# Gate stage of a two-block transformer step: two of four column groups of a scaled residual turned by VectorE block transposes in place of TensorE transposes

## The chip, the cores and the metric

The kernel runs on one core of a Trainium2 chip. The metric is the device time of one execution in microseconds; smaller is better. The times are medians of several runs. The profile is of one execution, taken by the hardware profiler.

## What is computed

The reference is two transformer blocks over a sequence of 256 positions of width 2048, in float32. The change lies in the last step of the first block, and in the norm with which the second block begins:

```python
# h: [1, 256, 2048] after the feed-forward of the first block
gate = jax.nn.sigmoid(rms_norm(h, norm_ple[i]) @ ple_w_gate[i])   # 2048 x 2048
h = h + (p[i] @ ple_w_proj[i]) * gate
...
x = rms_norm(h, norm_final)          # end of the first block
...
h = rms_norm_2(x, norm_g[i, 0])      # start of the second block
q, k, v = split_cols(h @ w_in, SWA_SPLITS)
```

`rms_norm` divides each row by the root of its mean square and multiplies by a gain for each column.

## The kernel before

**Precision.** A float32 product is made of three products of a shorter format: each weight piece `raw` is split into `whi` (a copy rounded by ScalarE, L2049) and `wlo = raw - whi` (VectorE, L1246), each activation into a high and a low half in the same way. TensorE then adds hi x hi, hi x lo and lo x hi (L604, L605, L606).

**Weight stream.** All weights come through one stream of 756 pieces of 128 x 1024 (512 KB), loaded by the SP queue into four slots (`SLOTS = 4`). A raw slot is loaded again once `wlo` of its piece is made (`lo_ready`). ScalarE's copy of a piece waits for its load and for TensorE to have used the piece four before (`piece_used`). VectorE's subtraction waits for ScalarE's copy (`hi_ready`), and TensorE waits for VectorE's (`lo_ready`) at a piece's first matmul.

**Order.** Each engine runs its own list of instructions in the order in which it is written. `rows_body` on VectorE and on ScalarE goes through a stage's pieces. In step q it splits piece q, then does what the dictionary `between` holds for q - LEAD (`LEAD = 3`), and then, on VectorE, if q - LEAD is the last piece of a group, it evacuates the group's two PSUM banks.

**The gate stage.** `rows_group` multiplies the 256 tokens (two tiles of 128) with 512 columns of `ple_w_gate` at a time: four column groups f, each of 8 pieces, each piece with 12 matmuls of 128 x 512. After group f ScalarE makes the sigmoid (`gate_sigmoid`), and VectorE's `gate_in` does three operations for each token tile: the sigmoid times the projection (L1795), plus the residual (L1796), and times the gain of the final norm into `xN` (L1798, it counts `ple_gain`). ScalarE then takes squares of both.

**Turning.** The next stage wants `xN` with the columns on the partitions. So each 128 x 512 column group of `xN`, with its two token tiles, is transposed to four tiles of 128 columns x 256 tokens. In the kernel before TensorE does this for all four groups, eight transposes each (`turn_gate`, `turn_rows`, L619), into four PSUM banks; group f - 1 is turned in the middle of gate group f. ScalarE (`tiles_hi`, L2087) and VectorE (`tiles_lo`, L1364) scale the turned tiles from PSUM by the second block's gain and split them into the halves of `H`. The next stage's values and keys are products with `H`.

The stage ahead, the last feed-forward product (`fd`), turns its column groups for f < 3 in another way: VectorE's `turn_quarters` moves 32 x 32 blocks from `xN` into `z`, 16 instructions in two lots of eight (L1373), one after the split of piece 8f + 11 and one after that of 8f + 12. `turned_hi` (L2093) and `turned_lo` (L1380) make the halves from `z`.

Of the kernel before, what the change touches and what calls it, by code (L numbers as in the profile page):

```python
# [209 lines left out]
def program(nc, xT, pT, wstream, consts, setup, params, grows, xrows, out):  # L210
# [11 lines left out]
    with ExitStack() as ctx:  # L222
        def sb(name, shape, dt=F32):
            return ctx.enter_context(nc.sbuf_tensor(name, shape, dt))

        def sem(name):
            return ctx.enter_context(nc.semaphore(name))
# [7 lines left out]
        H = sb("H", [P, CH, 2, S], FR)  # L235
# [88 lines left out]
        def gain(name, t):  # L324
            return par[:, ds(PO[name][0] + t, 1)]
# [4 lines left out]
        def part(buf, t, h):  # L330
# [45 lines left out]
        fd_sq, fd_turned, fd_hi, a2_ready = (sem(n) for n in ("fd_sq", "fd_turned", "fd_hi", "a2_ready"))  # L376
        grs_ready, ple_x, ple_gain, ple_sq, ple_turned, ple_hi, a3_ready = (
            sem(n) for n in ("grs_ready", "ple_x", "ple_gain", "ple_sq", "ple_turned", "ple_hi", "a3_ready"))
# [51 lines left out]
        def nsa_probs(n, e):  # L430

            _, _, e0, e1, probs = nsa_block(n)
            return probs.rearrange("p (r k b c) -> p r b k c", r=(e1 - e0) // 2, b=2, c=P // 2)[:, (e - e0) // 2, e % 2, :, :]
# [40 lines left out]
        def swa_out(buf, n, part):  # L474

            g, t, _, _, _ = swa_block(n)
            return buf[:, HPG * g:HPG * g + HPG, part, t * P:t * P + P]
# [37 lines left out]
        def _(pe):  # L515
# [74 lines left out]
            def rows_group(p, p0, u, u0, K, src, ready=None, between={}, upper=False, free=False):  # L590

                for t in range(QT):
                    if not free:
                        pe.wait_ge(z_ready, u + t + 1)
                for k in range(K):
                    if ready:
                        pe.wait_ge(*ready(k))
                    if k % 2 == 0:
                        pe.wait_ge(lo_ready, p + (k // 2 + 1))
                    s, w = (p0 + k // 2) % SLOTS, slice(k % 2 * WIDE, k % 2 * WIDE + WIDE)  # L600
                    for t in range(QT):
                        tok = slice(t * P, t * P + P)
                        bank = psum[(u0 + t) % 4 + (4 if upper else 0)]
                        nc.tensor.matmul(bank[:, :], src[:, k, 0, tok], whi[:, s, w], start=(k == 0), stop=False)  # L604
                        nc.tensor.matmul(bank[:, :], src[:, k, 0, tok], wlo[:, s, w], start=False, stop=False)  # L605
                        last = nc.tensor.matmul(bank[:, :], src[:, k, 1, tok], whi[:, s, w], start=False, stop=(k == K - 1))  # L606
                    if k % 2 == 1:
                        last.then_inc(piece_used, 1)
                        if k // 2 in between:
                            between[k // 2]()  # L610

            def turn_rows(f, lo_done, turned):

                if f:
                    pe.wait_ge(lo_done, 4 * f)
                for d in range(4):
                    for t in range(QT):
                        c = (4 * f + d) * P
                        last = nc.tensor.transpose(psum[4 + d][:, t * P:t * P + P], xN[:, t, c:c + P], ident)  # L619
                    last.then_inc(turned, 1)  # L620
# [356 lines left out]
            def turn_fd(f):  # L977

                pe.wait_ge(z_ready, 4 + UB["fd3"] + 2 * f + 2)
                turn_rows(f, a2_ready, fd_turned)  # L980
# [13 lines left out]
            def turn_gate(f):  # L994

                pe.wait_ge(ple_gain, 2 * f + 2)
                turn_rows(f, a3_ready, ple_turned)
            for f in range(4):
                rows_group(PB["gate"] + 8 * f, PB["gate"] + 8 * f, UB["gate"] + 2 * f, UB["gate"] + 2 * f, DT, A,
                           lambda k: (a2_ready, k + 1), {3: lambda: turn_gate(f - 1)} if f else {0: lambda: turn_fd(3)})  # L1000


            natural(PB["v2"], UB["v2"], H, {5: lambda: turn_gate(3)}, ready=lambda k: (a3_ready, k + 1))
# [236 lines left out]
        def _(dve):  # L1240
# [105 lines left out]
            def rows_body(p, p0, per, groups, evac, between={}, short=0, ahead={}, halves=()):  # L1346

                for q in range(LEAD, per * groups + AHEAD):
                    if q in ahead:
                        ahead[q]()  # L1350
                    if AHEAD <= q < per * groups + AHEAD - short:
                        split_lo(p + q, (p0 + q) % SLOTS, WIDE if q in halves else PW)
                    if q - LEAD in between:
                        between[q - LEAD]()
                    f, done = divmod(q - LEAD + 1, per)
                    if f and f <= groups and done == 0:
                        dve.wait_ge(piece_used, p + (SLOTS + q - LEAD + 1))
                        evac(f - 1)

            def tiles_lo(dst, name, f, hi_sem, ready):  # L1360

                for d in range(4 * f, 4 * f + 4):
                    dve.wait_ge(hi_sem, d + 1)
                    V.scalar_tensor_tensor(dst[:, d, 1, :], psum[4 + d % 4][:, 0:S], gain(name, d), dst[:, d, 0, :].bitcast(F32),  # L1364
                                           ALU.mult, ALU.subtract).then_inc(ready, 1)
# [10 lines left out]
            def turned_lo(dst, name, f, hi_sem, ready):  # L1376

                for d in range(4 * f, 4 * f + 4):
                    dve.wait_ge(hi_sem, d + 1)
                    V.scalar_tensor_tensor(dst[:, d, 1, :], z[:, d % 4, :], gain(name, d), dst[:, d, 0, :].bitcast(F32),  # L1380
                                           ALU.mult, ALU.subtract).then_inc(ready, 1)
# [70 lines left out]
            def nsa_lo(n):  # L1452

                g, t, _, _, _ = nsa_block(n)
                dve.wait_ge(nsa["o_hi"], 2 * g + 2 - t)
                V.tensor_tensor(swa_out(H, n, 1), psum[4 + t][:, :].rearrange("p (r q) -> p r q", r=HPG),
                                swa_out(H, n, 0).bitcast(F32), ALU.subtract).then_inc(nsa["o_ready"], 1)
# [303 lines left out]
            def fd_lo(f):  # L1761

                if f < 3:
                    turned_lo(A, "g_ple", f, fd_hi, a2_ready)
                else:
                    tiles_lo(A, "g_ple", f, fd_hi, a2_ready)
# [23 lines left out]
            def gate_in(f):  # L1790

                w = slice(f * WIDE, f * WIDE + WIDE)
                for t in range(QT):
# [3 lines left out]
                    dve.wait_ge(ple_x, 2 * f + t + 1)  # L1797
                    V.tensor_tensor(xN[:, t, w], yN[:, t, w], gfrow[:, w], ALU.mult).then_inc(ple_gain, 1)  # L1798

            def gate_lo(f):  # L1800

                tiles_lo(H, "g0", f, ple_hi, a3_ready)
            dve.wait_ge(in_gf, 16)
            rows_body(PB["gate"], PB["gate"], 8, 4, gate_in,
                      {2: lambda: fd_lo(3), 3: norm_gate, **{8 * f + 5: lambda f=f: gate_lo(f - 1) for f in range(1, 4)}})

            def norms_k2():

# [11 lines left out]
            def rows_k2():  # L1820

                take_rs(3, 4)
                V.tensor_scalar(rs2b, rs[:, :], float(HD) ** -0.5, None, ALU.mult).then_inc(rs_ready, 1)
            values(PB["v2"], UB["v2"], 0, nrs, {AHEAD + 1: lambda: gate_lo(3), AHEAD + 3: norms_k2})
            body(PB["k2"], PB["k2"], UB["k2"], UB["k2"], ZB["k2"], ZB["k2"], 4, DT, between={NORM_AT["k2"]: rows_k2})

# [212 lines left out]
        def _(act):  # L2039
# [35 lines left out]
            def rows_body(p, p0, it, pieces, between={}, short=0, halves=()):  # L2075

                for q in range(LEAD, pieces + AHEAD):
                    if AHEAD <= q < pieces + AHEAD - short:
                        split(p, p0, q, pieces, it, WIDE if q in halves else PW)
                    if q - LEAD in between:  # L2080
                        between[q - LEAD]()

            def tiles_hi(dst, name, f, turned, hi_sem):

                for d in range(4 * f, 4 * f + 4):
                    act.wait_ge(turned, d + 1)
                    C.activation(dst[:, d, 0, :], psum[4 + d % 4][:, 0:S], ACT.Copy, scale=gain(name, d)).then_inc(hi_sem, 1)  # L2087

            def turned_hi(dst, name, f, turned, hi_sem):

                act.wait_ge(turned, 4 * f + 4)
                for d in range(4 * f, 4 * f + 4):
                    C.activation(dst[:, d, 0, :], z[:, d % 4, :], ACT.Copy, scale=gain(name, d)).then_inc(hi_sem, 1)  # L2093
# [60 lines left out]
            g0, g1 = PO["g_mix"]  # L2154
# [197 lines left out]

            def gate_hi(f):

                tiles_hi(H, "g0", f, ple_turned, ple_hi)
            rows_body(PB["gate"], PB["gate"], 0, 32, {
                0: lambda: fd_squares(3), 1: lambda: fd_hi_of(3), 3: lambda: root(3, nrs, nvar),
                **{8 * f + 7: lambda f=f: gate_sigmoid(f) for f in range(4)},
# [129 lines left out]
            for c, n in enumerate(CHUNKS2):  # L2488
# [22 lines left out]
                else:  # L2511
# [6 lines left out]
                    for q in range(2 * n):  # L2518
                        if 2 <= q and q + LEAD < 2 * n:
                            split(PB[dn], PB[dn], q + LEAD, 0, 0)  # L2520
                        f, h = divmod(q, n // 2)
# [281 lines left out]
```

## Time and profile before

| | us |
|---|---|
| median of 3 runs | 2203.51 |
| lowest, highest | 2202.99, 2204.32 |
| the profiled execution | 2202.45 |
| its span in the profile | 2200.6 |
| TensorE busy | 2188.3 |
| VectorE busy | 1517.5 |
| ScalarE busy | 1123.5 |
| GpSimd busy | 628.7 |

The span runs from the first instruction of the program to the last; the execution's time holds 1.85 us around it. The gate stage stands at 1103.9 to 1194.6 us. Matmuls overlap in the engine, so the distance of their starts is the measure of TensorE's pace, and not their durations. In a row of a timeline, what stands in brackets is how long the engine was idle before, and what ended that.

### The profile page before, as it was taken

The numbers are of one execution on the slowest core, as the hardware profiler recorded it, in microseconds if no ns is written. First come the engines' busy times: TensorE is split into PE (matmuls) and PEld (weight loads), VectorE is DVE, ScalarE is ACT, GpSimd is POOL, SyncE is SP. The second block draws the span as 40 slices with busy tenths as digits, with TensorE's granted clock in tenths as the row PEclk, the third lists the DMA queues.
The fourth block names the chain that finished last, engine by engine and source line by source line (L and its number), as shares of the span: only waits on it lengthen the run. The fifth ranks groups of instructions, "written<-read, shape, count | busy, mean of one in ns | idle before, by whom it ended". The sixth has DMA issues, their size and how long they took to land.

```text
span 2200.6 us, 34123 instructions
## 1 busy us (share of the span) xinstructions
PE 2188.3 (99%) x11565; PEld 1870.8 (85%) x11565; DVE 1517.5 (69%) x2075; ACT 1123.5 (51%) x1690; POOL 628.7 (29%) x573
## 2 busy tenths in 40 slices
PE   9999999999999999999999999999999999999998
PEld 8888988888888888888888887888888888888887
DVE  6877765558658757755966666577774688756875
ACT  6445555555445445454556455465553455434553
POOL 3202320361362363153000133006540255303431
PEclk9999999999999999999999999999999999999999
DMA  7665335456555556555555653545555555555554
GB/s 253 232 228 170 107 133 187 169 185 213 189 186 206 191 181 209 201 200 191 186 187 192 220 174 134 198 157 187 194 191 194 188 191 191 191 191 191 189 209 147
DMA packets 118079, 414.28 MB, mean 188 GB/s; under 512 B 12897, under 2 KB 18049, under 8 KB 117473
## 3 DMA queue, kind: packets, MB, share of 16 engines
q1 hardware_dynamic: 111600, 401.37, 53.2%
q10 hardware_dynamic: 6384, 11.70, 1.7%
q8 instruction: 54, 0.88, 0.2%
q14 instruction: 41, 0.33, 0.0%
HBM read 409.29 MB, written 2.15 MB: 187 GB/s over the span
## 4 chain that ended last, share of the span: by engine, by line
PE 93%; POOL 2%; issue 2%; DVE 2%; ACT 1%; DMA 0%; POOLq 0%; DVEq 0%; ACTq 0%
PE bank L547 31%; PE bank L555 16%; PE bank L1207 4%; PE bank L1205 4%; PE bank L1206 4%; PE bank L881 4%; PE bank L882 4%; PE bank L883 4%; PE bank L605 3%; PE bank L606 3%; PE bank L604 3%; POOL bias L2544 1%; PE bank L660 1%; PE bank L661 1%; PE bank L662 1%
## 5 line engine op out<-in xcount | busy, mean ns | idle before, releaser
L1246 DVE TENSOR_TENSOR wboth<-raw,wboth 128x1024 fp32r<-128x1024 f32 x756 | 963.9, 1279 | 542.1 <-ACT wboth L2049 541.0
L2049 ACT CAST wboth<-raw 128x1024 fp32r<-128x1024 f32 x756 | 780.4, 1041 | 585.6 <-PE bank L1207 126.5
L547 PE MATMUL bank<-A,wboth 128*128 128x512 f32 x2928 | 705.4, 392 | 0.5 <-DVE wboth L1246 0.3
L547 PEld LDWEIGHTS bank<-A,wboth 128*128 128x128 f32 x2928 | 536.9, 188 | 105.2 <-issue 1.2
L555 PEld LDWEIGHTS bank<-A,wboth 128*128 128x128 f32 x2928 | 376.7, 191 | 14.8
L555 PE MATMUL bank<-A,wboth 128*128 128x256 f32 x2928 | 384.0, 283 | 0.0
L2544 POOL TENSOR_TENSOR PT<-z,rs 128x256 f32<-128x256 f32 x88 | 73.4, 835 | 465.8 <-DVE z L1277 465.2
L2544 POOL TENSOR_TENSOR bias<-z,rs 128x256 f32<-128x256 f32 x64 | 104.5, 1633 | 199.1 <-DVE z L1277 109.7
L1277 DVE TENSOR_REDUCE z<-bank 128x256 f32<-128x512 f32 x172 | 118.0, 687 | 28.2 <-PE bank L547 27.9
L1205 PE MATMUL bank<-wboth,H 128*128 128x512 f32 x352 | 136.9, 389 | 0.0
L1206 PE MATMUL bank<-wboth,H 128*128 128x512 f32 x352 | 136.9, 389 | 0.0
L1207 PE MATMUL bank<-wboth,H 128*128 128x512 f32 x352 | 136.9, 389 | 0.0
L881 PE MATMUL bank<-wboth,H 128*128 128x512 f32 x312 | 121.5, 389 | 1.2 <-DVE wboth L1246 1.2
L882 PE MATMUL bank<-wboth,H 128*128 128x512 f32 x312 | 121.4, 389 | 0.0
L883 PE MATMUL bank<-wboth,H 128*128 128x512 f32 x312 | 121.4, 389 | 0.0
L2262 ACT ACTIVATE Sm<-bias 128x256 f32<-128x256 f32 x64 | 26.7, 418 | 170.7 <-POOL bias L2544 170.7
L2630 POOL TENSOR_TENSOR x<-x,Sm 128x512 f32<-128x512 f32 x18 | 35.4, 1991 | 206.8 <-DVE x L1749 137.5
L2669 POOL TENSOR_TENSOR bias<-Sm 128x256 f32<-128x256 f32 x44 | 71.9, 1633 | 38.0 <-DVE Sm L1971 37.7
L2544 POOL TENSOR_TENSOR kT<-z,rs 128x256 f32 (+1 forms) x12 | 11.3, 942 | 249.9 <-DVE z L1277 249.9
L547 PE MATMUL bank<-H,wboth 128*128 128x512 f32 x320 | 79.1, 394 | 0.0
L1206 PEld LDWEIGHTS bank<-wboth,H 128*128 128x128 f32 x352 | 66.1, 188 | 13.8
L1207 PEld LDWEIGHTS bank<-wboth,H 128*128 128x128 f32 x352 | 66.1, 188 | 13.7
(340 smaller groups left out, 3090.3 us busy)
## 6 DMA issues: line engine op xcount, KB each, us to landing
raw<-wstream SPq DMA_DIRECT2D x756, 512.0 KB, 3.3
bias<-bias_rows ACTq DMA_DIRECT2D x6, 512.0 KB, 6.1
x<-xrows ACTq DMA_DIRECT2D x1, 2048.0 KB, 10.6
bias<-grows ACTq DMA_DIRECT2D x2, 1024.0 KB, 7.2
out<-x SPq DMA_DIRECT2D x8, 256.0 KB, 2.1
x<-xT SPq DMA_DIRECT2D x7, 256.0 KB, 5.4
pA<-bias_rows ACTq DMA_DIRECT2D x2, 512.0 KB, 8.8
Sm<-grows ACTq DMA_DIRECT2D x1, 1024.0 KB, 6.7
```

The costliest lines, as they stand in the source:

```text
L547: last = nc.tensor.matmul(bank(j)[:, :], whi[:, s, cols(i)], moving(j, k), start=(k == 0), stop=(k == K - 1))
L555: last = nc.tensor.matmul(bank(j)[:, 0:S], wlo[:, s, cols(i)], moving(j, k)[:, 0, :], start=False, stop=False)
L881: nc.tensor.matmul(bank[:, :], a_hi, w_hi, start=start, stop=False)
L882: nc.tensor.matmul(bank[:, :], a_hi, w_lo, start=False, stop=False)
L883: return nc.tensor.matmul(bank[:, :], a_lo, w_hi, start=False, stop=stop)
L1205: nc.tensor.matmul(bank[:, :], H[:, k, 0, tok], whi[:, s, w], start=(k == 0), stop=False)
L1206: nc.tensor.matmul(bank[:, :], H[:, k, 0, tok], wlo[:, s, w], start=False, stop=False)
L1207: return nc.tensor.matmul(bank[:, :], H[:, k, 1, tok], whi[:, s, w], start=False, stop=(k == n - 1))
L1246: V.tensor_tensor(wlo[:, s, 0:w], raw[:, s, 0:w], whi[:, s, 0:w].bitcast(F32), ALU.subtract).then_inc(lo_ready, 1)
L1277: V.tensor_reduce(dst(j) if dst else z[:, (z0 + j) % 4, :], bank[:, :].rearrange("p (h c) -> p c h", h=2), AX, ALU.add).then_inc(z_ready, 1)
L2049: C.copy(whi[:, s, 0:w], raw[:, s, 0:w]).then_inc(hi_ready, 1)
L2544: return lambda zz: G.tensor_tensor(dst, zz, by, ALU.mult)
```

## The change

The column groups f = 0 and 1 of the gate stage are turned by VectorE as in the stage ahead. TensorE's turns of these two go, its turns of groups 2 and 3 stay in their places, as does the turn of the feed-forward's fourth group (`turn_fd(3)`). VectorE gets two lots of eight block transposes for each of the two groups. ScalarE and VectorE read `z` for these groups in place of PSUM. `turned_hi` waits for all four tiles of a group at once.

```diff
@@ the tensor engine's list
             for f in range(4):
                 rows_group(PB["gate"] + 8 * f, PB["gate"] + 8 * f, UB["gate"] + 2 * f, UB["gate"] + 2 * f, DT, A,
-                           lambda k: (a2_ready, k + 1), {3: lambda: turn_gate(f - 1)} if f else {0: lambda: turn_fd(3)})
+                           lambda k: (a2_ready, k + 1), {0: {0: lambda: turn_fd(3)}, 3: {3: lambda: turn_gate(2)}}.get(f, {}))
@@ the vector engine's list
+            def gate_turn(f, i0):
+
+                if i0 == 0:
+                    dve.wait_ge(ple_gain, 2 * f + 2)
+                if f and i0 == 0:
+                    dve.wait_ge(a3_ready, 4 * f)
+                turn_quarters(f, i0, ple_turned)
+
             def gate_lo(f):
 
-                tiles_lo(H, "g0", f, ple_hi, a3_ready)
+                if f < 2:
+                    turned_lo(H, "g0", f, ple_hi, a3_ready)
+                else:
+                    tiles_lo(H, "g0", f, ple_hi, a3_ready)
             dve.wait_ge(in_gf, 16)
             rows_body(PB["gate"], PB["gate"], 8, 4, gate_in,
-                      {2: lambda: fd_lo(3), 3: norm_gate, **{8 * f + 5: lambda f=f: gate_lo(f - 1) for f in range(1, 4)}})
+                      {2: lambda: fd_lo(3), 3: norm_gate, **{8 * f + 8 + i: lambda f=f, i=i: gate_turn(f, 2 * i) for f in range(2) for i in range(2)}, **{8 * f + 5: lambda f=f: gate_lo(f - 1) for f in range(1, 4)}})
@@ the scalar engine's list
             def gate_hi(f):
 
-                tiles_hi(H, "g0", f, ple_turned, ple_hi)
+                if f < 2:
+                    turned_hi(H, "g0", f, ple_turned, ple_hi)
+                else:
+                    tiles_hi(H, "g0", f, ple_turned, ple_hi)
```

How the instructions stand, first on TensorE behind the twelfth piece of the gate stage (piece 11). `con` holds the identity, `x` is the memory of `xN`, `bank` a PSUM bank, `wboth` the split weights. Before:

```order
2582 L606 MATMUL bank<-wboth,A 128x512
2583 L619 MATMUL bank<-con,x 128x128 [waits ple_gain]
2584 L619 MATMUL bank<-con,x 128x128 x7
2585 L604 MATMUL bank<-wboth,A 128x512 [waits lo_ready,a2_ready]
2586 L605 MATMUL bank<-wboth,A 128x512
```

and now:

```order
2581 L605 MATMUL bank<-wboth,A 128x512
2582 L606 MATMUL bank<-wboth,A 128x512
2583 L604 MATMUL bank<-wboth,A 128x512 [waits lo_ready,a2_ready]
2584 L605 MATMUL bank<-wboth,A 128x512
2585 L606 MATMUL bank<-wboth,A 128x512
```

The eight transposes have gone from between two pieces; the matmul behind them, which waits for the split of its piece, stays.

On VectorE, behind the evacuation of gate group 0, whose last operation is L1798. Before:

```order
758 L1798 TENSOR_TENSOR x<-y,bias 128x512 [waits ple_x]
759 L1246 TENSOR_TENSOR wboth<-raw,wboth 128x1024 [waits hi_ready] x6
760 L1364 SCALAR_TENSOR_TENSOR H<-bank,par,H 128x256 [waits ple_hi] x4
761 L1246 TENSOR_TENSOR wboth<-raw,wboth 128x1024 [waits hi_ready] x2
```

and now:

```order
758 L1798 TENSOR_TENSOR x<-y,bias 128x512 [waits ple_x]
759 L1246 TENSOR_TENSOR wboth<-raw,wboth 128x1024 [waits hi_ready]
760 L1373 STREAM_TRANSPOSE z<-x 32x8x32 [waits ple_gain]
761 L1373 STREAM_TRANSPOSE z<-x 32x8x32 x7
762 L1246 TENSOR_TENSOR wboth<-raw,wboth 128x1024 [waits hi_ready]
763 L1373 STREAM_TRANSPOSE z<-x 32x8x32 x8
764 L1246 TENSOR_TENSOR wboth<-raw,wboth 128x1024 [waits hi_ready] x4
765 L1380 SCALAR_TENSOR_TENSOR H<-z,par,H 128x256 [waits ple_hi] x4
766 L1246 TENSOR_TENSOR wboth<-raw,wboth 128x1024 [waits hi_ready] x2
```

The six splits in a row are those of pieces 11 to 16. Eight transposes now stand between the first and the second of them, and eight between the second and the third. Behind the evacuation of group 1 it is the same with pieces 19 to 24.

## Rows read from the trace of the kernel before

**Rows 1.** The page: busy time of each engine, and the chain's shares by engine.

```profile
PE 2188.3 (99%) x11565; PEld 1870.8 (85%) x11565; DVE 1517.5 (69%) x2075; ACT 1123.5 (51%) x1690; POOL 628.7 (29%) x573
...
PE 93%; POOL 2%; issue 2%; DVE 2%; ACT 1%; DMA 0%; POOLq 0%; DVEq 0%; ACTq 0%
```

**Rows 2.** Busy us by window, in order PE, PEld, DVE, ACT, POOL; then clock, DMA.

```profile
1126.60:1149.20 22.60, 22.60 (x105) 18.80 (x104) 15.07 (x18) 14.56 (x23) 0.00 (x0) 1.00 0.55 185
```

**Rows 3.** Timeline, TensorE, gate stage: start us, us, engine, line, op, out<-in, count.

```profile
1109.82 0.39 PE L605 MATMUL bank<-wboth,A 128*128 128x512 f32 x1
...
1126.59 0.39 PE L604 MATMUL bank<-wboth,A 128*128 128x512 f32 x1
...
1137.02 0.39 PE L605 MATMUL bank<-wboth,A 128*128 128x512 f32 x1
1137.25 0.40 PE L606 MATMUL bank<-wboth,A 128*128 128x512 f32 x1
1137.48 1.04 PE L619 MATMUL bank<-con,x 128*128 128x128 f32 x8
...
1141.12 0.39 PE L604 MATMUL bank<-wboth,A 128*128 128x512 f32 x1
...
1149.28 0.39 PE L604 MATMUL bank<-wboth,A 128*128 128x512 f32 x1
```

**Rows 4.** Timeline, VectorE, last feed-forward product, group 0; L1373's durations (ns, min/median/max).

```profile
1038.86 1.28 DVE L1673 TENSOR_TENSOR x<-x,bank 128x512 f32<-128x512 f32 x2 [0.36 <-PE bank L606]
1040.06 1.22 DVE L1246 TENSOR_TENSOR wboth<-raw,wboth 128x1024 fp32r<-128x1024 f32 x1
1041.20 3.59 DVE L1373 STREAM_TRANSPOSE z<-x 32x256 f32<-32x256 f32 x8
1044.82 1.23 DVE L1246 TENSOR_TENSOR wboth<-raw,wboth 128x1024 fp32r<-128x1024 f32 x1
1046.07 3.60 DVE L1373 STREAM_TRANSPOSE z<-x 32x256 f32<-32x256 f32 x8
1049.71 2.36 DVE L1246 TENSOR_TENSOR wboth<-raw,wboth 128x1024 fp32r<-128x1024 f32 x2
...
L1373 DVE STREAM_TRANSPOSE z<-x x48: 425/436/442, 1041.2 to 1092.8; 32x256 f32<-32x256 f32 x48
```

**Rows 5.** Timeline, ScalarE, gate stage, between groups 0 and 1.

```profile
1126.84 1.28 ACT L2343 ACT_TABLE_LOAD   x1 [1.66 <-PE bank L606]
...
1137.73 1.05 ACT L2049 CAST wboth<-raw 128x1024 fp32r<-128x1024 f32 x1 [0.99 <-DMA raw<-wstream]
1138.69 1.56 ACT L2087 ACTIVATE H<-bank,par 128x256 fp32r<-128x256 f32 x4
```

**Rows 6.** Timeline, VectorE, gate stage: evacuation and splits behind groups 0 and 1.

```profile
1128.92 0.69 DVE L1795 TENSOR_TENSOR Sm<-Sm,y 128x512 f32<-128x512 f32 x1 [2.49 <-ACT Sm L2343]
...
1133.04 3.49 DVE L1246 TENSOR_TENSOR wboth<-raw,wboth 128x1024 fp32r<-128x1024 f32 x3
...
1150.32 0.69 DVE L1795 TENSOR_TENSOR Sm<-Sm,y 128x512 f32<-128x512 f32 x1 [1.20 <-ACT Sm L2343]
...
1154.43 3.49 DVE L1246 TENSOR_TENSOR wboth<-raw,wboth 128x1024 fp32r<-128x1024 f32 x3
```

**Rows 7.** Timeline, a pause of TensorE in the feed-forward: TensorE's rows, and VectorE's split.

```profile
500.64 0.39 PE L883 MATMUL bank<-wboth,H 128*128 128x512 f32 x1
...
500.94 1.22 DVE L1246 TENSOR_TENSOR wboth<-raw,wboth 128x1024 fp32r<-128x1024 f32 x1
...
502.21 0.50 PE L881 MATMUL bank<-wboth,H 128*128 128x512 f32 x1 [1.19 <-DVE wboth L1246]
...
505.11 0.39 PE L881 MATMUL bank<-Tboth,vT 128*128 128x512 f32 x1
```

**Rows 8.** Timeline, TensorE, near the start of the program.

```profile
8.79 0.63 PE L634 MATMUL bank<-wboth,A 128*128 128x512 f32 x1
9.21 0.63 PE L635 MATMUL bank<-wboth,A 128*128 128x512 f32 x1
```

## The prediction

> **What bounds the kernel now.** I read the page first: TensorE is busy for 99% of the span and owns 93% of the chain that ended last [rows 1]. So I went to the gate stage, which the change touches, and asked two things there: does TensorE ever pause, and how far ahead of it do the others run? The stretch of the second gate group, 1126.60 to 1149.20 us, shows TensorE busy for all of its 22.60 us at the full granted clock, VectorE for 15.07 and GpSimd for none [rows 2]. The timeline of TensorE gives the beat: from L605 at 1109.82 to L605 at 1137.02 lie ten weight pieces of 12 matmuls, 27.20 us with nothing between them, so a piece takes 2.72 us and a matmul 0.227 [rows 3]. The stage therefore ends when TensorE has issued its work. Whatever is taken off TensorE here is a gain in full, and whatever makes it pause is a loss in full, for no later stage has idle time of TensorE to give back.
>
> VectorE's 69% is an average and says little. What counts is how late its split of a piece (L1246, `wlo`) may come, since TensorE waits for it at that piece's first matmul. I number the gate pieces 0 to 31. VectorE runs three pieces ahead at a group's end: while it evacuates group 0 (pieces 0 to 7), pieces 8, 9 and 10 are ready, and the split of 11 comes after the evacuation.
>
> **Taken from TensorE.** Two runs of eight transposes go, after pieces 11 and 19. One costs this: from the L606 at 1137.25 to the L604 at 1141.12, the first of piece 13, are 3.87 us [rows 3], in which 13 matmul steps take 13 x 0.227 = 2.95. The rest, 0.92, is the price of a turn, with the slower matmuls that follow it. Two turns: **-1.84 us**. The third turn stays where it was.
>
> **Put on VectorE.** Each of the two column groups gets 16 block transposes (L1373), 8 behind the split of piece 8f+11 and 8 behind that of 8f+12. The stage before does the same thing in the same places, so its price is in the trace. VectorE's split starts at 1040.06, 8 transposes at 1041.20, the next split at 1044.82, 8 more at 1046.07, the split after at 1049.71 [rows 4]. If X is the start of the split of piece 11, then that of 12 starts at X + 4.76 and that of 13 at X + 9.65; each takes 1.22 us.
>
> The other half of the comparison is when X comes. In the stage before, the evacuation is two additions of 1.28 us together, which begin at 1038.86 as soon as the group is done. In the gate stage it is a sigmoid on ScalarE and six VectorE operations. For group 0 ScalarE first loads a table [rows 5], the six begin at 1128.92 [rows 6], and X is 1133.04, which is 6.45 us behind the start of piece 8 at 1126.59. For group 1, X is 1154.43, 5.15 us behind the start of piece 16 at 1149.28 [rows 3, 6]. After it stand three splits in a row, 3.49 us, with which VectorE now makes up what it fell behind; the transposes go into the middle of these.
>
> **The wait that comes.** I take from [rows 7] how TensorE behaves behind a late split: the split that began at 500.94 and took 1.22 ended at 502.16, and TensorE went on at 502.21, so 0.05 us later. The following 12 matmuls, from 502.21 to 505.11, took 2.90 in place of 2.72: restarting costs another 0.17.
>
> Group 0 turned. Split 12 ends at 1133.04 + 4.76 + 1.22 = 1139.02, TensorE would want it at 1126.59 + 4 x 2.72 = 1137.47: a first pause of 1.6 us. Split 13 ends at 1133.04 + 9.65 + 1.22 = 1143.91, so piece 13 starts at 1143.96; without pauses it would be 1126.59 + 5 x 2.72 = 1140.19. That is 3.77 late (the first pause is contained in it), with the restart **3.94 us**.
>
> Group 1 turned. Split 20 ends 5.15 + 4.76 + 1.22 = 11.13 us behind the start of piece 16, wanted at 10.88: a pause of 0.3. Split 21 ends at 5.15 + 9.65 + 1.22 = 16.02, piece 21 starts at 16.07 in place of 13.60: 2.47, with the restart **2.64 us**. Both offsets are counted from the group's own start, so the delay of group 0 doesn't change them.
>
> **What else moves.** The tiles for H: ScalarE now reads `z` and waits for all 16 transposes, which end at about 1142.7, before it scales them. In before it did so at 1138.69, between its casts of pieces 15 and 16 [rows 5]. The cast of 16 so comes at about 1144.4, and VectorE's split of 16 ends near 1147.4; TensorE will want piece 16 at about 1152.3. The load of a raw piece waits for the split of the piece four before: 16 is issued at 1139.0, and piece 15, whose predecessor's split ended at 1134.26, was cast at 1137.73, 3.5 us later. So 16 is there at 1142.5, in time. Both have about 5 us of cover and cost nothing; without it they would cost TensorE what they exceed it by. VectorE's waits before the transposes (for its own scaled residual, and for its own `a3` tiles of group 0) are on work it has finished. Behind the transposes on VectorE stand only splits until the four `H` operations, which no one needs before the next projection. Group 2's turn and group 3's are as they were. POOL and the SP queue get no new instruction.
>
> **The sum.** 3.94 + 2.64 - 1.84 = +4.74 us. Against the profiled execution's own 2202.45 (span 2200.6 and 1.85 around it): 2207.2. The median of the three runs is 1.06 above that execution, so I forecast **2208.3 us**, 0.22% slower.
>
> **A page that speaks to this.** The rows say 7.2 us of VectorE for eight 128x128 fp32 tiles, against 0.92 of TensorE. The Trainium skill, "VectorE: DVE Perf Modes", section "The three transpose paths", gives 311 ns for a 128x128 bf16 tile on VectorE, as 32x32 blocks only. An estimate by that page is 8 x 0.311 = 2.5 us for a group, and the chain to the last split would be 4.7 us shorter, so that both pauses vanish and the two removed turns are the whole effect. The trace's own rows are for this shape and type and go before. The same page, in "Rules for kernel authors", says to transpose 128x128 on TensorE if a PSUM destination will do, which speaks against this change.
>
> **Rivals.**
> 1. The transposes fit, nothing waits. This is what the stage before does: its split of 13 starts at 1049.71 with time to spare. It decides at X: the chain of 10.87 + 0.05 must end within 5 pieces, 13.60 us, so X may be at most 2.7 us behind the group's first matmul. The rows have 6.45 and 5.15, and ScalarE's sigmoid stands before. Then only -1.84 is left: **2201.7 us** on the median, not slower. Chance 0.05. The price of the page above leads to this same case.
> 2. The clock falls during the pauses. At the start of the program matmuls follow at 0.42 us (8.79 to 9.21 us) [rows 8], the 1.2 GHz level; after the pause of 1.35 us at 500.64 they did not [rows 7]. Now 2.0 us of pause come 2.9 us behind 1.6 us of it. If one piece in each group ran at the low level, 12 x (0.42 - 0.23) = 2.3 us twice: **2212.9 us**. The Trainium skill, "TensorE: Matmul & The Clock Gate", section "HAM oscillation", describes this fall for kernels in which TensorE waits between bursts; no row of before shows one. Chance 0.07.
> 3. A second chain is late. If ScalarE's wait for the turned tiles or the raw load took all of the 5 us of cover and 2 us more in each group, **2212 us**. For it: both are new and in a row on engines that serve TensorE. Against it: the margin above. Chance 0.05.
> 4. The pauses are shorter than worked out, because evacuation or transposes run quicker beside an idle TensorE: 1 us off in each group gives **2206.3**. Nothing in the rows does it. Chance 0.06.
>
> **How the numbers follow.** My forecast has 0.77. Its own uncertainty is about 0.5 us in the sum (the restart may be nil, -0.3; the offset X may shift by 0.2 in each group) and 0.5 to 0.8 in the runs, whose spread was 2202.99 to 2204.32; so 2207.1 to 2209.5. The range that should hold 8 in 10 takes in most of rival 4 and the lower part of rival 2: **2206.6 to 2210.4**. A measurement of this kernel can tell about 0.2% from no change, 4.4 us, that is 2207.9; the forecast lies only 0.4 above it. Of its 0.77 I give 0.50 to slower by over 0.2% and 0.27 to within it. With rivals 2 and 3 (0.12) slower has 0.62; with rivals 1 and 4 (0.11) same has 0.37; faster by over 0.2% would need 4.4 us where only 1.84 is removed: 0.01.
>
> **What would show it.** In the profile after, TensorE's L604 should show idle time ended by VectorE L1246 four times in the gate stage, of about 1.6, 2.0, 0.3 and 2.1 us (at the first matmul of pieces 12, 13, 20 and 21); L619 should have 56 matmuls; L1373 80 transposes of 425 to 442 ns as in [rows 4]; the first transposes should start at 1134.2; the granted clock of these stretches should stay 1.00. It is wrong if there is no idle time there (rival 1), if the matmul steps after a pause are 0.42 (rival 2), if ScalarE or a load is what piece 16 or 24 waits for (rival 3), or if TensorE pauses in another stage than before.

## The result

| | before | changed |
|---|---|---|
| median of 12 runs, us | 2203.04 | 2208.74 |
| lowest, highest | 2201.65, 2204.51 | 2206.49, 2211.07 |
| span of the profiled execution | 2200.6 | 2208.0 |
| gate stage: first L604 to first L660 | 1103.94 to 1194.62, 90.68 | 1104.86 to 1201.99, 97.13 |

The ratio is 1.0027, with a 95% interval of 1.0019 to 1.0034: slower by 5.7 us. The forecast was +4.7 us and 2208.3, with a range of 2206.6 to 2210.4, and 2208.74 lies inside. The profile's span grew by 7.4. The gate stage holds 6.45 of it. 0.92 us lie ahead of the stage, where nothing is changed: in this one execution the granted clock was 0.57 from 9 to 13 us, and TensorE's matmuls came every 0.43 us from 10.04 to 12.18, where in the trace of before they came every 0.23 from 10.21 on. The same matmul (L660) starts at 11.57 us there and at 12.57 here. Behind the stage both kernels need 1006.0 us to the end of the span. So all that follows is read as the length of the gate stage, from TensorE's first L604 with `A` to its first L660. This can be read to 0.05 us (two executions of the changed kernel give 97.13 and 97.11), where a median of a whole run can't.

### The profile page after: what moved, and what is told of

It reads as the page before. It is cut to its first block, busy times and chain, and to the rows that moved or that the text cites. A ratio compares the mean times of both kernels' runs of the same rounds, so it can differ in the third digit from the quotient of the medians.

```text
span 2208.0 us, 34123 instructions
## 1 busy us (share of the span) xinstructions
PE 2189.2 (99%) x11549; PEld 1870.1 (85%) x11549; DVE 1530.8 (69%) x2107; ACT 1123.5 (51%) x1690; POOL 628.4 (28%) x573
## 4 chain that ended last, share of the span: by engine, by line
PE 92%; DVE 3%; POOL 2%; issue 2%; ACT 1%; DMA 0%; POOLq 0%; DVEq 0%; ACTq 0%
PE bank L547 31%; PE bank L555 16%; PE bank L1207 4%; PE bank L1205 4%; PE bank L1206 4%; PE bank L881 4%; PE bank L883 4%; PE bank L882 4%; PE bank L604 3%; PE bank L606 3%; PE bank L605 3%; POOL bias L2558 1%; PE bank L660 1%; PE bank L661 1%; PE bank L662 1%
```

## The profile after

The page of the changed kernel, its busy times and the waits of TensorE over the whole span (who waited for whom: us in total, times, the longest):

```profile
PE 2189.2 (99%) x11549; PEld 1870.1 (85%) x11549; DVE 1530.8 (69%) x2107; ACT 1123.5 (51%) x1690; POOL 628.4 (28%) x573
...
PE 92%; DVE 3%; POOL 2%; issue 2%; ACT 1%; DMA 0%; POOLq 0%; DVEq 0%; ACTq 0%
...
PE bank L604 <- DVE wboth L1246: 5.6, 4, 1.9
PE bank L881 <- DVE wboth L1246: 1.2, 1, 1.2
```

The page alone would mislead: TensorE is still busy for 99%, with 16 instructions fewer. VectorE has 32 more instructions and 13.3 us more [rows 1], and its share is 69% as before. The share of VectorE in the chain, 3% in place of 2% [rows 1], and the first row of the waits give it away: L604 waits four times for VectorE's split, in a stage in which it had waited for nothing. The stretch that had 22.60 us of TensorE work and a clock of 1.00 [rows 2] now reads, with the columns as there:

```profile
1126.60:1149.20 22.60, 19.14 (x77) 15.09 (x76) 19.65 (x32) 12.58 (x21) 0.00 (x0) 0.92 0.37 120
```

TensorE has 77 instructions in it in place of 105, and the granted clock is 0.92. VectorE's timeline behind the evacuation of group 0, and ScalarE's halves of H:

```profile
1133.97 1.22 DVE L1246 TENSOR_TENSOR wboth<-raw,wboth 128x1024 fp32r<-128x1024 f32 x1
1135.10 3.59 DVE L1373 STREAM_TRANSPOSE z<-x 32x256 f32<-32x256 f32 x8
1138.72 1.23 DVE L1246 TENSOR_TENSOR wboth<-raw,wboth 128x1024 fp32r<-128x1024 f32 x1
1139.98 3.61 DVE L1373 STREAM_TRANSPOSE z<-x 32x256 f32<-32x256 f32 x8
1143.62 4.63 DVE L1246 TENSOR_TENSOR wboth<-raw,wboth 128x1024 fp32r<-128x1024 f32 x4
...
1143.62 1.71 ACT L2104 ACTIVATE H<-z,par 128x256 fp32r<-128x256 f32 x4 [3.92 <-DVE z L1373]
```

The splits start at X, X + 4.75 and X + 9.65 (X = 1133.97), as they do in the stage ahead [rows 4]; the three splits in a row of [rows 6] are torn apart. TensorE in the same time:

```profile
1127.52 0.39 PE L604 MATMUL bank<-wboth,A 128*128 128x512 f32 x1
...
1138.17 0.39 PE L606 MATMUL bank<-wboth,A 128*128 128x512 f32 x1
1140.10 0.47 PE L604 MATMUL bank<-wboth,A 128*128 128x512 f32 x1 [1.54 <-DVE wboth L1246]
...
1142.68 0.39 PE L606 MATMUL bank<-wboth,A 128*128 128x512 f32 x1
1144.99 0.47 PE L604 MATMUL bank<-wboth,A 128*128 128x512 f32 x1 [1.92 <-DVE wboth L1246]
1145.30 0.39 PE L605 MATMUL bank<-wboth,A 128*128 128x512 f32 x1
1145.52 0.42 PE L606 MATMUL bank<-wboth,A 128*128 128x512 f32 x1
1145.75 0.62 PE L604 MATMUL bank<-wboth,A 128*128 128x512 f32 x1
1146.17 0.63 PE L605 MATMUL bank<-wboth,A 128*128 128x512 f32 x1
...
1148.73 0.59 PE L605 MATMUL bank<-wboth,A 128*128 128x512 f32 x1
1149.16 0.40 PE L606 MATMUL bank<-wboth,A 128*128 128x512 f32 x1
...
1154.84 0.39 PE L604 MATMUL bank<-wboth,A 128*128 128x512 f32 x1
...
1171.02 0.47 PE L604 MATMUL bank<-wboth,A 128*128 128x512 f32 x1 [1.90 <-DVE wboth L1246]
```

Two things are to be seen. First the pauses. What stands in brackets is counted from the modelled end of the matmul before; the step between two starts, less the usual 0.23, is the time lost. It is 1.70 us ahead of piece 12 and 2.08 ahead of piece 13; piece 13 starts 17.47 us behind piece 8 (1127.52 to 1144.99), 3.87 more than five pieces of 2.72. In group 1 it is 0.40 and 2.06; piece 21 starts 16.18 behind piece 16 (1154.84 to 1171.02), 2.58 more than five pieces. Second the clock: from 1145.75 to 1149.16 stand eight steps of 0.427 in place of 0.227 us, the 1.2 GHz level, 1.6 us in all. With 0.09 of slower steps behind each of the two late starts the stage's account is 3.87 + 2.58 + 0.18 - 1.84 + 1.6 = 6.4 us; 6.45 were measured.

## The experiments

The theory is that VectorE's chain (the split of 11, eight transposes, the split of 12, eight more, the split of 13) is what TensorE waits for, because of where it stands. The rivals: other parts of the change cost time; gains and waits add up, so that the removed turns are worth something; VectorE has too much work in these groups wherever it stands. Beside these, the clock was open. All runs, with the stage read from each one's profile (a pause is a step between two starts less the usual one):

| run | median us | before beside it | ratio, 95% interval | gate stage us | pauses at pieces (us) | slow steps |
|---|---|---|---|---|---|---|
| changed kernel | 2208.74 | 2203.04 | 1.0027, 1.0019 to 1.0034 | 97.13 | 12: 1.70, 13: 2.08, 20: 0.40, 21: 2.06 | 8 |
| e1_turns_removed | 2200.39 | 2202.21 | 0.9993, 0.9983 to 1.0002 | 88.86 | none | 0 |
| e2_transposes_added | 2207.03 | 2202.21 | 1.0024, 1.0014 to 1.0034 | 95.58 | 12: 0.86, 13: 2.01, 21: 1.79 | 0 |
| e3_spread | 2200.19 | 2202.21 | 0.9991, 0.9982 to 1.0000 | 88.86 | none | 0 |
| e4_one_lot | 2208.60 | 2202.21 | 1.0030, 1.0019 to 1.0041 | 96.85 | 13: 3.74, 21: 2.46 | 7 to 8 |
| e5_only_group0 | 2206.15 | 2202.83 | 1.0016, 1.0007 to 1.0026 | 93.75 | 12: 1.70, 13: 2.07 | 0 |
| e6_only_group1 | 2204.81 | 2202.83 | 1.0010, 1.0000 to 1.0020 | 92.43 | 20: 0.40, 21: 2.09 | 0 |
| e7_changed_again | 2208.45 | 2202.83 | 1.0025, 1.0014 to 1.0036 | 97.11 | as the changed kernel's | 7 to 8 |
| e8_late_lots | 2204.54 | 2202.23 | 1.0010, 0.9999 to 1.0022 | 92.52 | 15: 0.70, 19: 0.78, 23: 0.96, 27: 0.81 | 0 |
| e9_late_eights | 2200.72 | 2202.23 | 0.9995, 0.9984 to 1.0006 | 88.86 | none | 0 |

**The turns taken away, nothing put in their place** (against the changed kernel):

```diff
-                turn_quarters(f, i0, ple_turned)
+                dve.sem_inc(ple_turned, 2)
```

> Neither engine turns column groups 0 and 1: TensorE's 16 transposes are gone and VectorE's 32 are not put in; the halves of H for these groups are made from what lies in z, so that part of the output is not computed. Theory (VectorE's chain of splits and transposes is what TensorE waits for): no pause in the gate stage, whose length from its first L604 to the first L660 falls from 90.68 us by the two turns, 1.84, to 88.84; the time is 0.08% below before. Rival (the rest of the change, such as reading z instead of PSUM or ScalarE's wait for all four tiles, costs time too): the stage is longer than 88.9.

The stage runs from 1103.67 to 1192.53: 88.86 us. That is 1.82 less than before, the worth of two turns. So reading `z` in place of PSUM costs nothing. This run doesn't test the single wait for four tiles, since `ple_turned` is counted here before ScalarE asks for it; in the changed kernel ScalarE waits 3.92 us there, and TensorE still pauses at none of the pieces 14 to 19.

```profile
1103.67 0.39 PE L604 MATMUL bank<-wboth,A 128*128 128x512 f32 x1
...
1192.53 0.39 PE L660 MATMUL bank<-wboth,H 128*128 128x512 f32 x1
```

**The transposes added to the kernel before**, TensorE's turns kept:

```diff
             rows_body(PB["gate"], PB["gate"], 8, 4, gate_in,
-                      {2: lambda: fd_lo(3), 3: norm_gate, ...
+                      {2: lambda: fd_lo(3), 3: norm_gate, **{8 * f + 8 + i: lambda f=f, i=i: gate_turn(f, 2 * i) for f in range(2) for i in range(2)}, ...
```

> The kernel before with the 32 block transposes added on VectorE in the changed kernel's places; their result is used by no one, TensorE still turns all groups. Theory: the split of piece 13 (21) ends at the same time as in the changed kernel, whether TensorE turns or not, so TensorE's turn only shortens the pause. Pauses of about 1.7, 1.2, 0.4 and 1.2 us, and the stage is as long as in the changed kernel but for the clock: 90.68 + 4.8 = 95.5 us. The two turns that the change takes away then gave nothing. Rival (the gain of the removed turns and the pauses add up): the stage is 1.84 us longer than the changed kernel's 95.5, so 97.3.

```profile
1137.24 1.04 PE L619 MATMUL bank<-con,x 128*128 128x128 f32 x8
1138.89 0.47 PE L604 MATMUL bank<-wboth,A 128*128 128x512 f32 x1 [0.61 <-DVE wboth L1246]
...
1143.75 0.47 PE L604 MATMUL bank<-wboth,A 128*128 128x512 f32 x1 [1.85 <-DVE wboth L1246]
```

The stage is 95.58 us, and the changed kernel's without its eight slow steps is 97.13 - 1.6 = 95.5. The turn stands here between pieces 11 and 12 and fills the first part of the wait; the first matmul behind it is 0.86 us late all the same (0.61 in the row's brackets), and piece 13 comes when VectorE lets it. So the removed turns gave the changed kernel nothing: the rival's 97.3 is out. The split of the waits I had wrong: 1.7 and 1.2 us expected in group 0, 0.86 and 2.01 measured. The turn shortens the wait in which it stands and not the one behind. In group 1 it is longer than the wait of 0.40 at piece 20, and the next pause is 0.27 shorter for it. The end is the same: piece 21 starts 16.29 us behind piece 16, in the changed kernel 16.18.

**The same instructions in other places.** Lots of four behind the splits of pieces 14 to 17, and the halves of H behind them:

```diff
-                turn_quarters(f, i0, ple_turned)
+                turn_quarter(f, i0, ple_turned)      # one i of the loop in turn_quarters: 4 transposes
...
-            **{8 * f + 8 + i: lambda f=f, i=i: gate_turn(f, 2 * i) for f in range(2) for i in range(2)}, **{8 * f + 5: lambda f=f: gate_lo(f - 1) for f in range(1, 4)}})
+            **{8 * f + 11 + i: lambda f=f, i=i: gate_turn(f, i) for f in range(2) for i in range(4)}, 17: lambda: gate_lo(0), 25: lambda: gate_lo(1), 29: lambda: gate_lo(2)})
...
-                **{8 * f + 4: lambda f=f: gate_hi(f - 1) for f in range(1, 4)}})
+                16: lambda: gate_hi(0), 24: lambda: gate_hi(1), 28: lambda: gate_hi(2)})
```

> The changed kernel with VectorE's transposes in lots of four behind the splits of pieces 14 to 17 (and 22 to 25) in place of lots of eight behind 11 and 12 (19 and 20), and with the making of the halves of H for these groups moved behind them (ScalarE's steps 16 and 24, VectorE's 17 and 25). The same instructions on every engine. Theory (it is the place of the lots, not their work): no pause of TensorE in the stage, 88.84 us long, time 0.08% below before, 0.35% below the changed kernel. Rival (VectorE has too much work in these groups wherever it stands: 15.1 us and 7.2 in each of 21.8 us): pauses of at least 0.5 us per group remain, at pieces 19 and 27.

VectorE's timeline of this kernel, behind the evacuation of group 0:

```profile
1132.43 3.49 DVE L1246 TENSOR_TENSOR wboth<-raw,wboth 128x1024 fp32r<-128x1024 f32 x3
1136.16 1.23 DVE L1246 TENSOR_TENSOR wboth<-raw,wboth 128x1024 fp32r<-128x1024 f32 x1 [0.25 <-ACT wboth L2068]
1137.31 1.77 DVE L1381 STREAM_TRANSPOSE z<-x 32x256 f32<-32x256 f32 x4
1139.11 1.22 DVE L1246 TENSOR_TENSOR wboth<-raw,wboth 128x1024 fp32r<-128x1024 f32 x1
1140.37 1.78 DVE L1381 STREAM_TRANSPOSE z<-x 32x256 f32<-32x256 f32 x4
...
1148.34 1.23 DVE L1246 TENSOR_TENSOR wboth<-raw,wboth 128x1024 fp32r<-128x1024 f32 x1
1149.48 0.69 DVE L1803 TENSOR_TENSOR Sm<-Sm,y 128x512 f32<-128x512 f32 x1
```

VectorE first makes up its three splits. Then a split and four transposes take 3.06 us (1137.31 to 1140.37), more than the 2.72 of a piece, but it has lead to spend, and the next evacuation starts at 1149.48. TensorE doesn't pause.

How much lead a piece has can be read from e1, where nothing is turned: the split of piece 12 ends 2.08 us before TensorE starts that piece (1135.12 and 1137.20), that of 13 3.67 us before, that of 14 4.92. In the changed kernel one lot of eight puts the split of 12 back by 4.76 - 1.14 = 3.62 us, and two put that of 13 back by 9.65 - 2.27 = 7.38. With TensorE's 0.15 us behind a late split that makes 3.62 - 2.08 + 0.15 = 1.69 us at piece 12 and 7.38 - 3.67 + 0.15 = 3.86 at piece 13; 1.70 and 3.87 were measured. In e3 a little of the delay reaches the next evacuations: the split of piece 19 ends 1.10 us ahead of its use where it has 1.77 in e1, that of piece 27 0.45 where it has 1.77. There isn't much room left.

The stage is 88.86 us, the same as with no turning at all: 16 transposes of TensorE saved, 32 on VectorE hidden whole. It is the place, not the amount. The median is 2.0 us below before, with an interval of 0.9982 to 1.0000 that only just reaches no change; by the two ratios, 0.9991 and 1.0027, it is 0.36% below the changed kernel.

**One lot of 16 per group**, behind the split of piece 12 (20):

```diff
-            **{8 * f + 8 + i: lambda f=f, i=i: gate_turn(f, 2 * i) for f in range(2) for i in range(2)}
+            **{8 * f + 9: lambda f=f: [gate_turn(f, 0), gate_turn(f, 2)] for f in range(2)}
```

> The changed kernel with the 16 transposes of a group in one lot behind the split of piece 12 (20) in place of eight behind 11 and eight behind 12. The split of 13 ends when it did, so TensorE has one pause of about 3.7 us (group 0) and 2.4 us (group 1) in place of two each. Theory of the waits: the stage is as long as the changed kernel's without its clock loss, 95.5 us. On the clock: if one long pause lets it fall as two in a row did, there are matmul steps of 0.43 us behind the pause of group 0, and perhaps of group 1, 1.6 us each; if two pauses with work between them were needed, there are none.

```profile
1139.31 0.39 PE L606 MATMUL bank<-wboth,A 128*128 128x512 f32 x1
1143.28 0.57 PE L604 MATMUL bank<-wboth,A 128*128 128x512 f32 x1 [3.58 <-DVE wboth L1246]
1143.65 0.63 PE L605 MATMUL bank<-wboth,A 128*128 128x512 f32 x1
...
1146.64 0.52 PE L606 MATMUL bank<-wboth,A 128*128 128x512 f32 x1
...
1169.20 0.47 PE L604 MATMUL bank<-wboth,A 128*128 128x512 f32 x1 [2.30 <-DVE wboth L1246]
```

The stage is 96.85 us; seven steps of 0.427 and two partly slow ones (0.37 and 0.36) take 1.6 us of it, and 95.2 remain, for 95.5 in the changed kernel. The pauses add up in two (3.74 + 2.46 = 6.20) to nearly what they did in four (3.87 + 2.58 = 6.45). The clock fell behind the pause of 3.74 us, and not behind that of 2.46.

**One group each.** The lot of group 0 or of group 1 alone, TensorE's turn put back for the other (`2: {3: lambda: turn_gate(1)}` or `1: {3: lambda: turn_gate(0)}`), and the halves of H made from PSUM for that one:

```diff
-            **{8 * f + 8 + i: lambda f=f, i=i: gate_turn(f, 2 * i) for f in range(2) for i in range(2)}
+            **{8 * f + 8 + i: lambda f=f, i=i: gate_turn(f, 2 * i) for f in (0,) for i in range(2)}
```

> Column group 0 turned by VectorE as in the changed kernel, group 1 by TensorE as in the kernel before. Theory of the waits: pauses of 1.7 and 2.1 us at pieces 12 and 13 with the restart 3.94, less one turn of 0.92: the stage is 90.68 + 3.0 = 93.7 us without clock loss, and up to 1.6 us more where the clock falls behind the second pause. No pause in the group after. Rival (the groups are not independent; the delay of group 0 made that of group 1): more than 93.7 without low steps.

> Column group 1 turned by VectorE as in the changed kernel, group 0 by TensorE as in the kernel before. Theory of the waits: pauses of 0.4 and 2.1 us at pieces 20 and 21, with the restart 2.64, less one turn of 0.92: the stage is 90.68 + 1.7 = 92.4 us, no matmul step of 0.43. Group 0 costs more than group 1 by 1.3 us, which is ScalarE's table load ahead of the first sigmoid. Rival (the groups are not independent): the pauses are of another length than in the changed kernel.

93.75 and 92.43 us, for 93.7 and 92.4 expected; the pauses are those of the changed kernel to 0.03 us, and 3.07 + 1.75 = 4.82 is the changed kernel's loss without the clock. So the groups are independent, and group 0 costs 1.3 us more. That is the 1.30 us by which X comes later behind its first matmul, and ScalarE's table load ahead of group 0's sigmoid took 1.28 us [rows 5]; no run moves that load. In the first of the two, TensorE went on behind the same two pauses at the full level:

```profile
1140.92 0.39 PE L606 MATMUL bank<-wboth,A 128*128 128x512 f32 x1
1143.22 0.47 PE L604 MATMUL bank<-wboth,A 128*128 128x512 f32 x1 [1.91 <-DVE wboth L1246]
1143.53 0.39 PE L605 MATMUL bank<-wboth,A 128*128 128x512 f32 x1
1143.76 0.40 PE L606 MATMUL bank<-wboth,A 128*128 128x512 f32 x1
1143.99 0.40 PE L604 MATMUL bank<-wboth,A 128*128 128x512 f32 x1
```

**The changed kernel a second time**, for the clock.

> The changed kernel itself, a second look for the clock. The pauses are 1.7, 2.1, 0.4 and 2.1 us again. If the fall of the clock behind the first two follows from the pauses alone, there are again 8 matmul steps of 0.43 us, and the stage is 97.1 us; if it depends on something that differs between executions, it may lie between 95.5 (none) and 98.7 (both groups).

97.11 us, the same pauses, the clock at the low level again for seven whole steps and a part of two. Of three executions in which pauses of 1.7 and 2.1 us stood in group 0, the clock fell in two. In the three in which 0.4 and 2.1 stood in group 1 it fell in none.

**The lots two pieces later, all else in place:**

```diff
-            **{8 * f + 8 + i: lambda f=f, i=i: gate_turn(f, 2 * i) for f in range(2) for i in range(2)}
+            **{8 * f + 10 + i: lambda f=f, i=i: gate_turn(f, 2 * i) for f in range(2) for i in range(2)}
```

> The changed kernel with its two lots of eight behind the splits of pieces 13 and 14 (21 and 22) in place of 11 and 12 (19 and 20), all else as it was; ScalarE still waits for the turned tiles between its casts of pieces 15 and 16. Worked out piece by piece with the durations of the trace: VectorE is level with ScalarE before the lots, so no pause at pieces 12 and 13; but the halves of H and the evacuation behind them come late, and short pauses of 0.4 to 0.9 us are left at pieces 15, 19, 23 and 27. The stage is 92.3 us, 1.6 more than before and 3.2 less than the changed kernel without clock loss (theory: place decides, and the place of the halves too). Rival (only the lots' place decides): no pause, 88.9.

```profile
1144.56 1.23 DVE L1246 TENSOR_TENSOR wboth<-raw,wboth 128x1024 fp32r<-128x1024 f32 x1
1147.24 1.23 DVE L1246 TENSOR_TENSOR wboth<-raw,wboth 128x1024 fp32r<-128x1024 f32 x1 [1.46 <-ACT wboth L2060]
...
1137.32 1.05 ACT L2060 CAST wboth<-raw 128x1024 fp32r<-128x1024 f32 x1 [0.99 <-PE bank L606]
1144.56 1.71 ACT L2104 ACTIVATE H<-z,par 128x256 fp32r<-128x256 f32 x4 [6.19 <-DVE z L1373]
1146.17 2.94 ACT L2060 CAST wboth<-raw 128x1024 fp32r<-128x1024 f32 x3
```

92.52 us for 92.3 expected, with small pauses at the four pieces that were named. No pause is left at 12 and 13. The pause at 15 is still the lots' own: the split of 15 starts at 1144.56, right behind the second lot, 6.18 us after its cast was ready. But ScalarE now stands for 6.19 us in front of the halves of H, its casts of 16, 17 and 18 come in a row behind, and VectorE, which had caught up, waits 1.46 us for the first of them; the next evacuation and the split of 19 come late. So a second place seems to matter for the pauses at 19 and 27, that of the wait for the turned tiles in ScalarE's list. This is read from the trace: no run moves that wait and leaves the lots here.

**Lots of eight with the halves late:** gate_turn at 8f + 11 and 8f + 13, `gate_hi` and `gate_lo` as in the spread kernel (the edit is against that kernel, with `turn_quarters` again in place of `turn_quarter`).

```diff
-            **{8 * f + 11 + i: lambda f=f, i=i: gate_turn(f, i) for f in range(2) for i in range(4)}
+            **{8 * f + 11 + 2 * i: lambda f=f, i=i: gate_turn(f, 2 * i) for f in range(2) for i in range(2)}
```

> As the spread kernel of the third experiment (halves of H at the same late steps), but in lots of eight behind the splits of pieces 14 and 16 (22 and 24). Theory: the size of a lot is no matter where VectorE has lead enough: no pause, 88.9 us. Rival (lots of eight are too long beside a split in any place): pauses of about 1 us per group and over 90 us.

88.86 us, no pause: behind the splits of 14 and 16 (22 and 24) lots of eight cost as little as lots of four.

## Why the prediction was right

- *TensorE bounds the stage and gives no idle time back.* Right: behind the stage both kernels take 1006.0 us.
- *A turn is worth 0.92 us.* Right: two are worth 1.82 (e1). But in the changed kernel their removal bought nothing, since it falls into a wait (e2). My sum handled that correctly as arithmetic, because the pauses were counted against a kernel without the turns; the sentence that whatever is taken off TensorE is a gain in full was too strong.
- *VectorE's chain is X, X + 4.76, X + 9.65.* Measured 4.75 and 9.65.
- *X stands 6.45 and 5.15 us behind the group's first matmul.* Measured 1133.97 - 1127.52 = 6.45, and 5.16 (1160.00 - 1154.84).
- *Group 0 loses 3.94, group 1 loses 2.64.* Measured 3.87 + 0.09 and 2.58 + 0.09. The parts were off in opposite ways: TensorE went on 0.15 us behind the end of the split and not 0.05, and restarting cost 0.09 and not 0.17. My row for both was one pause in another stage [rows 7].
- *Cover of ScalarE's wait and the raw load.* Right: neither was exceeded. ScalarE waited 3.92 us for the tiles and then cast piece 16 without a wait for its load, and the split of 16 still ended 5.0 us before TensorE started the piece, in the execution without a clock loss (e5). With a wait of 6.19 us, in e8, 0.27 us are left.
- *The clock.* Rival 2 had 0.07 and happened in part: group 0 at 8 steps, 1.6 us, where I had written 12 steps in each group. By the prediction's own signs this was one of being wrong: the granted clock was to stay at 1.00, and no matmul step behind a pause was to be 0.42. The chance was too low. The first pauses follow one another closely, and the only pause of over 0.4 us in the trace of before, behind its first 10 us, was a single one of 1.35. Nearly the whole distance between the forecast +4.7 and the stage's 6.45 is this term; between the forecast and the medians' +5.7 it is 1 us, which is what a fall in some executions and not in others would give. Each execution's mean granted clock is on record to three places: the four of the twelve with 0.999 took 2206.49 to 2208.57 us, the eight with 0.998 or 0.997 took 2207.65 to 2211.07. That agrees, but it doesn't tell where in the program the clock fell, so the share is argued and not shown.
- *The counts and the start.* Right: L619 has 56 matmuls, L1373 80 transposes, and the first of these in the gate stage starts at 1135.10, which is 1134.18 without the 0.92 us ahead of the stage.
- *The number.* 2208.3 lies nearer to 2208.74 than +4.7 does to +5.7, and that is luck: the forecast stood on a median of 2203.51 for before, and the twelve runs gave 2203.04.
- *The price from the page.* The estimate from the Trainium skill's 311 ns for a 128x128 bf16 tile ("VectorE: DVE Perf Modes", "The three transpose paths") led to rival 1's 2201.7. The trace has 16 transposes in 7.2 us for eight tiles in float32, 0.9 us a tile. The measurement decides. The same page of the Trainium skill says in "Rules for kernel authors" to use TensorE for a 128x128 transpose if a PSUM destination will do. The changed kernel agrees with that, at 6.45 us more in the stage; e3 doesn't, where VectorE turns the same tiles and the stage is 1.82 us shorter than before.

## What to carry to other kernels

When work is moved from a saturated engine to one with idle time, look for the place and not for the share: add up from which moment the second engine is late, and by how much its next delivery may slip before the first one waits. Here VectorE was 69% busy. Against the kernel in which nothing turns these groups (88.86 us), the same 32 instructions cost 8.3 us right behind an evacuation, 1.6 of them by the clock, and nothing three pieces later. Look also at the consumer that waits in order for the moved work (ScalarE's halves): in the two kernels without a loss it was moved too. And count a removed instruction as a gain only if its engine does not wait at that spot anyway.

## What the runs showed of the hardware

- Short pauses of TensorE can cost the clock too: behind 1.7 and 2.1 us with 2.8 us of work between, it fell to 1.2 GHz for 7 to 8 matmul steps in two of three executions, and behind one of 3.74 us in the one execution. It did not fall behind one of 2.46 us (e4, group 1), nor behind pauses of 1.8 to 2.1 us with 0.9 us or less at the piece before. Near the start of the program, where the code is the same, the granted clock was 0.57 over 9 to 13 us in one execution of the changed kernel and 1.00 in the one of before. What tells the executions apart is open. Each fall cost about 1.6 us.
- TensorE started 0.15 us (0.14 to 0.15) behind the end of the split that it waited for, at every pause of the gate stage in these runs (in e8, 1145.78 to 1145.93); one pause in the trace of before had 0.05.
- Block transposes on VectorE took the same time (424 to 443 ns) in lots of 4, 8 and 16, beside a busy or a waiting TensorE.
